# Fourth column pair of two feed-forward down projections: from one half of the tokens after the other to seven products, with one product of the third pair moved behind it

## What is computed

```python
def swiglu(u, w_gate, w_up, w_down):
    return (jax.nn.silu(u @ w_gate) * (u @ w_up)) @ w_down

u = modulate(rmsnorm(h, g_ff1), sh1, sc1)
h = h + FFN_RES * gt1[:, None, :] * swiglu(u, w1_gate, w1_up, w1_down)
u = modulate(rmsnorm(h, g_mix), sh2, sc2)      # what follows the first one
...
h = h + FFN_RES * gt3[:, None, :] * swiglu(u, w2_gate, w2_up, w2_down)
return rmsnorm(h, g_final)                     # and the second one; the second block norms again
```

## Time and profile before

| | |
|---|---|
| median of 3 runs | 1179.72 us (1178.71 to 1181.79) |
| profiled execution, first to last instruction | 1177.4 us |
| TensorE busy | 1164.3 us, 99% |
| VectorE, ScalarE, GpSimd busy | 737.2, 352.1, 86.2 us |
| first down projection, on TensorE | 162.3 to 234.5 us |
| second down projection, on TensorE | 695.6 to 768.0 us |

### The profile page before, as it was taken

One profiled execution on the slowest core, in us unless ns is written; L12 is line 12 of the kernel. 1 busy time (PEld: TensorE's weight loads), 2 busy tenths in 40 slices (PEclk: granted clock), 3 DMA queues, 4 the chain that ended last, 5 costly groups with the idle time before them and its releaser, 6 DMA issues.

```text
span 1177.4 us, 21319 instructions
## 1 busy us (share of the span) xinstructions
PE 1164.3 (99%) x8862; PEld 1076.8 (91%) x8862; DVE 737.2 (63%) x1658; ACT 352.1 (30%) x996; POOL 86.2 (7%) x104
## 2 busy tenths in 40 slices
PE   9999999999999999999999999999999999999997
PEld 7889999998878999999999999988888998888887
DVE  4558888675148866982898888567845231167632
ACT  2111210232124555212321210245333431056542
POOL 0000000200011000022000000310004010001111
PEclk9999999999999999999999999999999999999999
DMA  9969949762655457676599759574524643642311
GB/s 344 366 217 321 315 154 313 290 245 90 219 180 187 150 214 259 236 264 231 185 342 304 235 201 294 193 260 171 146 61 144 215 144 114 187 136 73 117 63 36
DMA packets 164272, 241.78 MB, mean 205 GB/s; under 512 B 14033, under 2 KB 112559, under 8 KB 164176
## 3 DMA queue, kind: packets, MB, share of 16 engines
q1 hardware_dynamic: 156256, 230.45, 57.9%
q10 hardware_dynamic: 6784, 5.74, 1.7%
q0 software_dynamic: 1136, 4.22, 1.1%
HBM read 236.82 MB, written 4.62 MB: 205 GB/s over the span
## 4 chain that ended last, share of the span: by engine, by line
PE 91%; DVE 5%; DMA 2%; ACT 1%; issue 1%; POOL 0%; DVEq 0%; ACTq 0%
PE ps L189 89%; PE ps L192 2%; DVE arena L198 2%; DMA slots<-in_w_proj_a 1%; DVE x L198 1%; DMA slots<-in_w_proj_b 1%; ACT U L195 1%; DVE slots L207 1%; ACT tmps L195 0%; DVE arena L204 0%; DVE rstd L216 0%; DVE tmps L204 0%; DVE slots L198 0%; DVE tmps L198 0%; POOL arena L198 0%
## 5 line engine op out<-in xcount | busy, mean ns | idle before, releaser
L189 PE MATMUL ps<-U,slots 128*128 128x128 f32 (+2 forms) x2800 | 478.7, 330 | 0.0
L189 PEld LDWEIGHTS ps<-U,slots 128*128 128x128 f32 (+1 forms) x2800 | 419.7, 190 | 40.7 <-issue 4.7
L189 PE MATMUL ps<-arena,slots 128*128 128x128 f32 (+1 forms) x1776 | 237.6, 294 | 0.0
L189 PEld LDWEIGHTS ps<-arena,slots 128*128 128x128 f32 x1776 | 225.3, 192 | 8.6 <-issue 0.4
L195 ACT ACTIVATE tmps<-ps 128x256 f32<-128x256 f32 (+2 forms) x151 | 57.4, 383 | 343.4 <-PE ps L189 319.4
L207 DVE CUSTOM_DVE_ANT_0 arena<-arena,tmpA 128x1024 f32<-128x1024 f32 x96 | 118.2, 1275 | 19.3 <-DMA arena<-in_w_adaT 19.1
L195 ACT ACTIVATE arena<-ps 128x256 f32<-128x256 f32 (+3 forms) x150 | 59.5, 416 | 155.9 <-PE ps L189 152.1
L189 PE MATMUL ps<-arena 128*128 128x128 f32 (+7 forms) x940 | 101.9, 287 | 0.9 <-DVE arena L198 0.9
L189 PEld LDWEIGHTS ps<-arena 128*128 128x128 f32 (+2 forms) x940 | 92.4, 181 | 9.8 <-issue 4.2
L189 PE MATMUL ps<-ABT,arena 128*128 128x128 f32 (+5 forms) x752 | 81.9, 271 | 0.0
L189 PEld LDWEIGHTS ps<-ABT,arena 128*128 128x128 f32 (+3 forms) x752 | 72.5, 174 | 0.8 <-issue 0.8
(11 more groups left out here) (199 smaller groups left out, 1140.6 us busy)
## 6 DMA issues: line engine op xcount, KB each, us to landing
slots<-in_w_in SPq DMA_DIRECT2D x14, 2048.0 KB, 10.3
slots<-in_w_down SPq DMA_DIRECT2D x16, 1408.0 KB, 9.8
slots<-in_w_gate SPq DMA_DIRECT2D x18, 1024.0 KB, 8.0
slots<-in_w_up SPq DMA_DIRECT2D x18, 1024.0 KB, 10.8
arena<-in_w_adaT SPq DMA_DIRECT2D x36, 512.0 KB, 6.1
arena<-in_ada_w1T SPq DMA_DIRECT2D x24, 512.0 KB, 7.5
slots<-in_a_in_w SPq DMA_DIRECT2D x6, 2048.0 KB, 9.8
slots<-in_b_in_w SPq DMA_DIRECT2D x12, 1024.0 KB, 5.4
```

Of the source, the lines that this page charges most:

```text
L189: return Nothing() if self.e is None else self.e.matmul(*a, **k)
```

## The change

Pair 3 goes through `t_dn` as well, in both feed-forward parts, with six of its products in the order p1, p2, p6, p5, p3, p7, and then p4 of pair 2 (held back, with the half-0 sums behind its sixth matmul), and then p4 of pair 3. Its copies and squares are interleaved on ScalarE (`s_downs_end`), its parts reach `H` through `v_dn_early`, `v_dn_half0`, `v_dn_c22` and `v_dn_c21`. `late` falls from 3 to 2 for n2 and n4. The sums of n2 and n4 get a PSUM bank of their own. VectorE also makes the four weight sums of pair 3, while it handles pair 2, and in the first part the last three ada chunks move behind the residual of half 1.

```diff
-            return {"n1": 4, "n2": 3, "n3": 2, "n4": 3, "n5": 2, "no": 2}[tag]
+            return {"n1": 4, "n2": 2, "n3": 2, "n4": 2, "n5": 2, "no": 2}[tag]
...
         def t_dn(e, f, p):
...
+            dn_product(e, A[:, 0:P], t2, SD[:, 1]).then_inc(*pe.up(n, "p6", p))
+            dn_product(e, C2[:, P:T], t1, SD[:, 0]).then_inc(*pe.up(n, "p5", p))
+            if p < 3:
+                t_dn_p7(e, f, p)
+            e.wait_ge(*act.at(n, "s5", p))
+            dn_product(e, C2[:, P:T], hi[:, :, P:T], SD[:, 3]).then_inc(*pe.up(n, "p3", p))
+            W.close([pe.now(), dve.at(n, "t4", p)], n, 2 * p + 1)
+            if p < 2:
+                t_dn_p4(e, f, p)
...
         def t_downs(e, f, tag):
...
-            for p in range(3):
+            for p in range(4):
                 t_dn(e, f, p)
             for x in free_of(Q, 1):
                 e.wait_ge(*x)
-            t_down(e, f, 3, 0)
-            t_down(e, f, 3, 1, amid={(1, 0): first_sums})
+            t_dn_p7(e, f, 3)
+            t_dn_p4(e, f, 2, amid=lambda e: t_sums_half(e, tag, 0))
+            t_dn_p4(e, f, 3)
...
+        def s_downs_end(e, f, tag):
+
+            s_squares_early(e, tag)
+            s_dn_step(e, f, 3, 0)
+            s_square(e, tag, 2, 0)
+            s_dn_step(e, f, 3, 1)
+            s_dn_step(e, f, 3, 2)
+            s_square(e, tag, 3, 0)
+            s_dn_step(e, f, 3, 3)
+            s_root(e, tag, 0, squares=False)
...
             for p in range(3):
-                if p < 2:
-                    v_dn_t1(e, "f1", p + 1)
+                v_dn_t1(e, "f1", p + 1)
                 v_ada_chunks(e, DCHUNKS[p])
...
                 v_dn(e, "f1", p, sm[:, 96:104], "n1")
             v_ada_chunks(e, DCHUNKS[3][:5])
-            v_residual(e, "f1 dn", 3, sm[:, 96:104], "n1", 0)
-            v_ada_chunks(e, DCHUNKS[3][5:])
+            v_dn_early(e, "f1", sm[:, 96:104], "n1")
+            v_dn_half0(e, "f1", sm[:, 96:104])
+            v_dn_c22(e, "f1", sm[:, 96:104])
             v_root(e, "n2", 0)
             v_normed(e, "n2", 0)
-            v_residual(e, "f1 dn", 3, sm[:, 96:104], "n1", 1)
+            for p in (2, 3):
+                v_dn_c21(e, "f1", p, sm[:, 96:104])
+            v_ada_chunks(e, DCHUNKS[3][5:])
             v_root(e, "n2", 1)
```

More of the change, by code:

```diff
@@ L691, in s_root @@
             hs = span(half)
-            ps = X.buf("sums", tag, 0 if half is None else half)
+            r = sums_ring(tag)
+            ps = r.buf("sums", tag, 0 if half is None else half)
             e.wait_ge(*pe.at("sums", tag, 1 if half is None else half))
@@ L697, in s_root @@
                 e.activation(RF[:, hs], ps[:, 0:P], ACT.Sqrt, bias=eps, scale=1.0 / D).then_inc(*act.up("sqrt f", half))
-                X.close([act.now()], "sums", tag, half)
+                r.close([act.now()], "sums", tag, half)
             elif half is None:
@@ L721, in p_squares @@
         def p_squares(e, tag):
+            if late(tag) == 0:
+                for half in range(2):
+                    acc, sq = sq_acc(tag, "sq")[:, HALF[half]], TC.buf("sq", tag, 0, half)
+                    e.wait_ge(*act.at("sq", tag, 0, half))
+                    e.tensor_tensor(acc, sq[:, 0:P], sq[:, P:T], ALU.add).then_inc(*pool.up())
+                    TC.close([pool.now()], "sq", tag, 0, half)
+                    for c2 in range(1, 4):
+                        p_squares_late(e, tag, "sq", c2, half)
+                return
             for c2 in range(1, late(tag)):
@@ L827, in t_sums_half @@
         def t_sums_half(e, tag, half):
-            ps, free = X.open("sums", tag, half)
+            ps, free = sums_ring(tag).open("sums", tag, half)
             for f in free:
@@ L865, in v_root @@
             if tag == "n4":
-                ps = X.buf("sums", tag, half)
+                ps = sums_ring(tag).buf("sums", tag, half)
                 e.wait_ge(*pe.at("sums", tag, half))
@@ L992, in v_gate @@
             gu_ring(f, c).close([dve.now()], f, "gu", c, half)
-        def t_down(e, f, p, half=None, amid=None):
-            ps, free = L.open(f + " dn", p, *by_half(half))
-            for w in free:
-                e.wait_ge(*w)
-            m = T if half is None else P
-            for j in range(2):
-                for h in range(2):
-                    e.wait_ge(*arrived(f + " dn", 2 * p + h))
-                    (wv,) = w_of(f + " dn", 2 * p + h)
-                    for k in range(11):
-                        c = 11 * h + k
-                        if amid and (j, c) in amid:
-                            amid[j, c](e)
-                        e.wait_ge(*dve.at(f, "act", c))
-                        i = e.matmul(ps[:, j * m:(j + 1) * m], wv[:, k, j * P:(j + 1) * P], actT[:, c, span(half)], start=c == 0, stop=c == 21)
-            i.then_inc(*pe.up(f + " dn", p, *by_half(half)))
-            if half != 0:
-                for h in range(2):
-                    W.close([pe.now()], f + " dn", 2 * p + h)
         SETS = [(psum[:, i:i + 2, :], psum[:, i + 2:i + 4, :]) for i in (4, 0)]
@@ L1185, in v_dn_t1 @@
             lo, hi = dn_of(f, p)
[L1186 removed]
+            e.wait_ge(*(pe.at(f, "p4", 9) if p == 0 else pe.at(f, "p4", 10) if p == 1 else pe.at(f + " dn", "p4", p - 2)))
             e.wait_ge(*arrived(f + " dn", 2 * p))
@@ L1207, in v_dn_t34, with dn_product @@
             e.tensor_tensor(t4, hi[:, :, 0:P], t2, ALU.subtract).then_inc(*dve.up(f + " dn", "t4", p))
+        def dn_product(e, out, stationary, moving, start=False, ready=None, amid=None):
+            for k in range(11):
+                if ready is not None:
+                    e.wait_ge(*ready(k))
+                if k == 6 and amid is not None:
+                    amid(e)
+                i = e.matmul(out, stationary[:, k, :], moving[:, k, :], start=start and k == 0, stop=k == 10, skip_group_check=True)
+            return i
         def t_dn(e, f, p):
```

112 lines of the change are left out of this document (68 added, 44 removed).

## The result

The changed kernel is slower: 1188.54 us as the median of four runs (1186.18 to 1189.23) against 1180.76 of the kernel before on the same chip (1178.71 to 1182.39), a ratio of 1.0058 with a 95% interval of 1.0044 to 1.0072. I had forecast 1180.7 in a range of 1178.0 to 1183.0, so the time lies 5.5 us above the range and on the side to which I had given 0.10. The profiled execution's span is 1184.4 us, 7.0 more than before; each profile is of the fastest of these executions. Three single executions of later runs that took 1608.56 to 2429.56 us are left out of every ratio.

The account below looks back on a forecast made before the run. TensorE, busy 1164.3 of 1177.4 us, was taken as the bound. Waits for GpSimd leave the first part 0.05 and the second 0.92 us slower: span 1178.4, median 1180.7, range 1178.0 to 1183.0.

Parts of the forecast that it names:

- the side to which I had given 0.10: Measured time slower than 1183.3 us, the late-load rival and a bit; chance 0.10.
- What is removed, and the copy: Pair 3 on TensorE: 2.46 us less work per part, 0.53 us of new wait for copy s5 before p3.
- VectorE and half 0, first part: VectorE forms t1 at 203.94, starts half 0's residual at 225.2; sums wanted at 228.80 have 1.3 us to spare.
- The load xm 0: First part, before the next projection: issued at 223.45, landing at 233.75, so TensorE waits 1.15 us.
- GpSimd and half 1, first part: Two of GpSimd's four operations slowed beside chunks; half-1 sums at about 238.15, the first part 0.05 us slower.
- GpSimd and half 1, second part: Eight GpSimd operations instead of four delay the half-1 sums: 0.92 us slower, bounds 0.7 and 1.3.
- have 0.8 us or more to spare: Second part: weight loads and ada chunks have at least 0.8 us of slack.
- Behind the sums of half 1 the rows of both kernels are the same work.: After the half-1 sums: same work in both kernels, with no term added to the forecast.
- Rival (d): TensorE's clock falls during 3.1 us of waiting in the second part, costing 0.9 us: 1181.6; chance 0.11.
- the five cases: Main forecast, half-1 sums bound by GpSimd in both parts, chance 0.60, and four rivals.
- Rival (c): Load of "dn" 6 lands later, delaying the sums of both halves: 1184.8 us; chance 0.09.
- rival (b): Half 1's chains hide and both parts gain 1.93 us: 1175.9; chance 0.05.

Follow-up runs that it names:

- The single edit with the chunks moved: Changed kernel with the second part's four ada chunks moved from ahead of the fourth pair's residual to behind the norm of half 1: ratio 1.0062, span 1184.9 us.
- the run with two empty uses: Changed kernel with two empty uses of PSUM ring L added at the fourth pair in each part: ratio 1.0041 to the kernel before, span 1183.3 us.
- the first part alone: Kernel before with the change in the first feed-forward part only: ratio 1.0035, span 1180.8 us.
- the five mends: Changed kernel with ring L kept, xm 0 earlier, moved chunks behind half 1's norm, n4's weighted squares on VectorE, pair 2's squares early: ratio 1.0002, span 1177.6 us.
- the second alone: Kernel before with the change in the second feed-forward part only: ratio 1.0013, span 1180.9 us.

## Why the prediction was wrong, by its own steps

**The size of the miss.** The median is 7.8 us above my 1180.7, the span 6.0 above my 1178.4. The other 1.8 is the base: the median of before, over four executions, is 1180.76 and not 1179.72, and the medians lie 0.8 further apart than the profiles. Two steps of the prediction failed and make up nearly all of the 6.0: the second part, 2.1 where I had 0.92, and the work behind the half-1 sums, 4.2 where I had nothing.

**What is removed, and the copy.** Right for the most part. The products take what they took. p3 starts 5.44 behind p6 (217.41 to 222.85), which is two products and the 0.53 that I had for the copy s5; 0.37 of it is listed as idle. The restart behind the wait costs 0.1 more (p3 and p7 in 5.02 for 4.91), for which I had no term, here or at the other waits. "The other copies lie a full product ahead of their use" failed by 0.2 us once, for s1 in the second part.

**VectorE and half 0, first part.** Right: t1 of pair 3 at 205.04 (203.94 forecast; 0.3 of the difference is from the start, the rest from its weight load, issued at 195.30 and not 194.04), the residual of half 0 at 225.64 (225.2), no wait at the sums.

**The load xm 0.** Right in kind, 1.88 where I had 1.15. It was issued at 224.25, not 223.45, and landed 10.8 later.

**GpSimd and half 1, first part.** Near in the number, 0.3 slower where I had 0.05, but not bound by GpSimd as forecast: the half-1 sums start without a wait, 3.67 behind the load. Two of four operations were slowed (1.10 and 1.31), as assumed, and GpSimd was done at 238.49, 0.2 ahead of them. With the load early the wait for GpSimd came out of its cover (1.80), so both ends lay within 0.2. My own sum had a slip: 234.70 and four operations (1.94) with the 1.24 extra end at 237.88, not 238.1, which is 0.2 faster than before and not 0.05 slower; with all four slowed it would be 1.1 slower, not 0.9.

**GpSimd and half 1, second part.** The step failed by its size, 2.1 where I had 0.92 and a bound of 1.3. Eight operations in 3.8 us were right, and so was the place. What failed is the last sentence there, that the weight loads and chunks of that part "have 0.8 us or more to spare". I had allowed for contention in the first part and not in the second, where VectorE's fourth sum of weights took 2.70 and its chunks 1.47, and GpSimd's operations of half 0 up to 1.44. The residual of half 0 came 1.3 late instead of having 0.8 to spare, the sums waited 0.45, and so did the whole chain of half 1 behind them. The single edit with the chunks moved took this away again.

**"Behind the sums of half 1 the rows of both kernels are the same work."** This sentence failed worst: it put at nothing what measured 4.2 us. The work is the same and the times aren't, for three reasons. The bank that the attention scores wait for is named by number, and the change moves the ring under it: 1.5 us, shown by the run with two empty uses and by the absence of the wait with one part alone. The diff had told it, since the fourth pair no longer takes its two tiles from that ring; I didn't follow the ring behind the place of the change. The load of `w_proj_b` near 507 cost 0.9 to 1.3 more in the profiles of the changed kernel, of the first part alone and of the five mends, and nothing with the second alone; in all twelve profiles with the first part changed it lands in 11.4 to 11.9 us, in the three without in 10.3 to 10.7. Why stays open: its issue keeps its place in TensorE's work, and no run moved it from there. And the clock, 1.6 us.

**Rival (d), the clock.** I gave it 0.11 and 0.9 us, and argued from the earlier trace rows that a stretch of 2 us without a matmul had kept 0.98. It came in both profiles of the changed kernel, behind GpSimd's waits in the second part, and cost 1.62; with the ring's turn kept it came in the first part too, behind a wait of 2.57 for the load, and cost 1.63. The row at the kernel's end was misread. Its 0.98 in place of 1.00 is the start of a fall, as the stretch behind it in the same trace of before shows:

```profile
1175.00:1177.00 2.00, 0.00 (x0) 0.00 (x0) 0.00 (x0) 0.00 (x0) 0.00 (x0) 0.50 0.78 226
```

The price was low as well: I had 0.22 us lost per us at 0.50, from the row at the kernel's start, and 23 records for 38 in 4 us are some 0.4 per us. The waiting itself was 2.9 us by my own two pieces, not 3.1. Here the Trainium skill (TensorE: Matmul & The Clock Gate, What's actually happening) was nearer with its drop to 1.2 GHz after idleness than my reading of the row. But the runs don't show that idleness of this length is enough: with the second part alone the same waits of 1.98 and 0.46 stand in the profile, and the block behind takes 15.54.

**The chances.** 0.10 for slower rested on a late load alone. Late VectorE, the ring's turn and the slower load, which each hurt by 1 to 1.5 us, had no place in it, and the clock was in rival (d) at 0.9 in place of 1.6. All of them go to the same side, because TensorE hardly waited there before. Of the five cases the forecast was nearest in its mechanism, but GpSimd bound the half-1 sums in the second part only. Rival (c)'s cause didn't come: the load of "dn" 6 was there 9.7 us after its issue. With everything late mended, rival (b)'s gain exists up to the half-1 sums of the first part (1.85 of 1.93), and is then spent at loads and at VectorE.

## What to carry to other kernels

Where one engine is busy 99% of the time, count work taken off it as a gain only up to the next thing that it waits for, and look for that thing behind the change as well: loads, rings of buffers named by number, and the next users of the other engines. Work that is moved beside other work on VectorE and GpSimd costs its slowed time, in every part where the two meet and not only in the one that looks tight. A new wait of about 2 us on a TensorE that never waited has to be priced with the clock that may fall behind it.

## What the runs showed of the hardware

The fifteen profiles that were read have 20 waits of TensorE of 1.7 to 2.6 us inside a full stretch. Eight were followed by a spell at 0.50, at a cost of 1.6 us beside the wait (17.16 for 15.54, 5.47 for 3.84): the wait of 1.98 in the second part in five of six profiles, and single ones of 2.03, 2.15 and 2.57. Twelve were followed by none: all eight of 1.71 to 1.88, and one each of 1.98, 2.03, 2.20 and 2.49. So the length of the wait alone doesn't tell. VectorE and GpSimd slow each other by more than I had allowed: 1.62 became 2.70 for a sum over 1408 elements beside a GpSimd operation on 512 elements, which itself took 2.13 to 2.43 in the two profiles of the changed kernel where the first of its kind took 1.29 in the profile before, and 0.46 became 1.44 on 128x128. This agrees with the Trainium skill (GPSIMD Engine Reference, Key points) on shared SBUF interfaces; the sizes are the runs'. One 2 MB load took 10.3 to 10.7 us in one form of the kernel and 11.4 to 11.9 in the other, at much the same rate of traffic around it (370 and 367 GB/s in the third and fourth us behind its issue, 384 to 394 and 385 to 387 after that), for a cause that I haven't found.
